# Last output projection of a two-layer decoder trunk: 512 weight columns per matmul instead of 256

## The reference

```python
def branch_b(h, w_in, w_out):
    z = h @ w_in
    q, k, v, gate = jnp.split(z, [B_WIDTH, 2 * B_WIDTH, 3 * B_WIDTH], axis=-1)
    o = stick_breaking_attention(q, k, v).astype(h.dtype)
    return (o * jax.nn.silu(gate)) @ w_out
...
def reference(x, meta_tokens, rel_bias, w_in_a, sinks_a, w_out_a, w_in_b, w_out_b, ln_g, ln_b):
    ...
    h = jnp.concatenate([meta, x], axis=1)
    for i in range(DEPTH):
        j = i // N_MIXERS
        if i % N_MIXERS == 0:
            y = branch_a(h, w_in_a[j], sinks_a[j], w_out_a[j], rel_bias)
        else:
            y = branch_b(h, w_in_b[j], w_out_b[j])
        h = layer_norm(DEEPNORM_ALPHA * h + y, ln_g[i], ln_b[i])
    return h[:, N_META:]
```

## Time and profile before

| what | us |
|---|---|
| median of 3 runs | 966.68 |
| lowest and highest | 965.02, 967.41 |
| span of the profiled execution | 963.3 |
| last output projection, first to last matmul, in that span | 857.8 to 952.4 |
| from the last matmul to the end of the span | 10.9 |

### The profile page before, as it was taken

The page is one execution under the profiler, slowest core; times in us unless marked ns, Lnnn a source line. Parts: engine busy times, 40 slices in busy tenths (PEclk is TensorE's granted clock), DMA queues, the critical chain, the costliest instruction groups (busy, mean ns, idle before and its releaser), DMA issues.

```text
span 963.3 us, 18988 instructions
## 1 busy us (share of the span) xinstructions
PE 928.8 (96%) x7592; PEld 891.9 (93%) x7592; DVE 554.6 (58%) x721; ACT 436.2 (45%) x716; POOL 64.1 (7%) x88
## 2 busy tenths in 40 slices
PE   5999999999999999898999999999999999999995
PEld 5998999999998999898999999999999999999995
DVE  4466566567555666696736455454545546455556
ACT  5456555455645433345445353445335353543330
POOL 2220232032010000011000000000000000000000
PEclk9999999999999999989999999999999999999998
DMA  8755653564343344413554443434344343444532
GB/s 280 237 154 183 210 154 119 149 204 134 129 163 132 131 175 175 175 45 132 195 181 149 152 152 139 166 133 175 132 169 174 131 168 137 174 152 178 206 119 88
DMA packets 24595, 152.99 MB, mean 159 GB/s; under 512 B 3392, under 2 KB 3408, under 8 KB 7792
## 3 DMA queue, kind: packets, MB, share of 16 engines
q1 hardware_dynamic: 20736, 140.52, 40.3%
q0 software_dynamic: 2960, 7.63, 4.1%
q10 hardware_dynamic: 864, 4.33, 1.2%
HBM read 150.28 MB, written 2.18 MB: 158 GB/s over the span
## 4 chain that ended last, share of the span: by engine, by line
PE 88%; DVE 5%; DMA 3%; ACT 1%; issue 1%; SPq 0%; DVEq 0%; ACTq 0%
PE bank L245 72%; DMA raw<-chunks 3%; PE bank L333 2%; PE bank L534 2%; DVE w_lo L820 2%; PE bank L294 2%; ACT w_hi L558 1%; PE bank L314 1%; PE bank L450 1%; PE bank L399 1%; DVE h L1056 1%; PE bank L416 0%; PE bank L405 0%; PE bank L447 0%; PE bank L309 0%
## 5 line engine op out<-in xcount | busy, mean ns | idle before, releaser
L245 PE MATMUL bank<-x_hi,w_hi 128*128 128x272 f32 (+1 forms) x1536 | 446.2, 291 | 16.1 <-DVE w_lo L840 10.4
L245 PE MATMUL bank<-x_hi,w_lo 128*128 128x272 f32 (+1 forms) x1536 | 441.5, 287 | 0.0
L245 PE MATMUL bank<-x_lo,w_hi 128*128 128x272 f32 (+1 forms) x1536 | 441.2, 287 | 0.0
L820 DVE TENSOR_TENSOR w_lo<-raw,w_hi 128x2048 fp32r<-128x2048 f32 x130 | 303.4, 2339 | 218.8 <-ACT w_hi L558 218.6
L558 ACT ACTIVATE w_hi<-raw 128x2048 fp32r<-128x2048 f32 x130 | 248.3, 1911 | 214.3 <-PE bank L245 122.7
L245 PEld LDWEIGHTS bank<-x_hi,w_hi 128*128 128x128 f32 x1536 | 291.6, 190 | 22.4 <-DVE x_lo L826 10.9
L245 PEld LDWEIGHTS bank<-x_hi,w_lo 128*128 128x128 f32 x1536 | 291.2, 190 | 0.0
L245 PEld LDWEIGHTS bank<-x_lo,w_hi 128*128 128x128 f32 x1536 | 291.0, 189 | 0.0
L245 PE MATMUL bank<-og_hi,w_hi 128*128 128x272 f32 x256 | 74.9, 293 | 0.3 <-DVE og_lo L927 0.3
L245 PE MATMUL bank<-og_hi,w_lo 128*128 128x272 f32 x256 | 74.1, 289 | 0.0
L245 PE MATMUL bank<-og_lo,w_hi 128*128 128x272 f32 x256 | 73.7, 288 | 0.0
(11 more groups left out here) (199 smaller groups left out, 1042.0 us busy)
## 6 DMA issues: line engine op xcount, KB each, us to landing
raw<-chunks SPq DMA_DIRECT2D x130, 1024.0 KB, 4.8
work<-bias_table POOLq DMA_DIRECT2D x8, 512.0 KB, 5.8
work<-bias_table POOLq DMA_DIRECT2D x8, 256.0 KB, 6.8
work<-ln_rows ACTq DMA_DIRECT2D x1, 2048.0 KB, 8.2
out<-work SPq DMA_DIRECT2D x8, 256.0 KB, 2.4
h<-xT ACTq DMA_DIRECT2D x3, 544.0 KB, 12.4
raw<-chunks SPq DMA_DIRECT2D x4, 256.0 KB, 7.6
raw<-chunks SPq DMA_DIRECT2D x2, 512.0 KB, 14.1
```

The costliest lines, as they stand in the source:

```text
L245: last = mm(o, l, r, start=(kt == 0 and n == 0), stop=(kt == KT - 1 and n == 2))
L820: V.tensor_tensor(w_lo[:, slot, :, :], raw[:, half, :, :], w_hi[:, slot, :, :].bitcast(f32), ALU.subtract).then_inc(lo_ready, 1)
```

## The change

The last output projection is tiled as 4 rows of 512 output columns (`RW`) in place of 8 pairs of 256. A chunk now holds 4 contraction tiles x 512 columns; its size, its slots and SP's program stay. A row is 4 chunks (c = 0 to 3), and for each chunk PE runs both token tiles: 12 matmuls of 512 columns each, 24 for a chunk, 96 for a row, 384 for the stage. A new semaphore `quarter_used` tells ACT that chunks 0 to 2 of a row are used up; for chunk 3 it is `tile_full[1]`. The transposes of the residual stand after chunk 1 of row 0, that is after 48 matmuls of 512 columns, where they stood after 48 of 256.

DVE makes one add and one statistics instruction of 512 columns for a row and token tile. Its order for row j is now: low parts of chunks 0, 1 and 2 of row j + 1, then `out_cols` of row j for both tiles, then the low part of chunk 3. The last row (j = 3) goes to banks 2 and 3, one for each token tile, tile by tile as before.

```diff
+RW = 512
+QUARTER = KT // 4
+ROW_ITERS = D // RW
...
-        bn_out = sb("bn_out", [128, 2, D // CW, 6])
+        bn_out = sb("bn_out", [128, 2, ROW_ITERS, 6])
...
-        last_acc = (bank[2:4], bank[4:6])
+        last_acc = bank[2:4]
...
+            def row_quarter(j, c, u, o):
+                for k in range(QUARTER):
+                    kt = QUARTER * c + k
+                    whi, wlo = (w[:, c].rearrange("p a b -> p (a b)")[:, k * RW:(k + 1) * RW] for w in (w_hi, w_lo))
+                    part = slice(u * 128, u * 128 + 128)
+                    terms = ((og_hi, whi), (og_lo, whi), (og_hi, wlo))
+                    for n, (m, w) in enumerate(terms):
+                        last = mm(o, m[:, kt, part], w, start=(kt == 0 and n == 0), stop=(kt == KT - 1 and n == 2))
+                return last
+            def out_rows(j):
+                for c in range(4):
+                    pe.wait_ge(lo_ready, 2 * P_OUT_B + 4 * j + c + 1)
+                    for u in range(2):
+                        if c == 0:
+                            pe.wait_ge(tile_free[u], P_OUT_B + j)
+                        last = row_quarter(j, c, u, acc[u][:])
+                        if c == 3:
+                            last.then_inc(tile_full[u], 1)
+                        elif u == 1:
+                            last.then_inc(quarter_used, 1)
+                    if c == 1 and isinstance(j, int):
+                        residual_rows()
             pe.wait_ge(og_lo_ready, O_A + HALF)
-            project(P_OUT_B, og_hi, og_lo, None, token_major=True, between=residual_rows)
-            project(P_OUT_B + 1, og_hi, og_lo, None, token_major=True)
-            with pe.Fori(1, 3) as j:
-                for p in range(2):
-                    project(P_OUT_B + 2 * j + p, og_hi, og_lo, None, token_major=True)
-            for u in range(2):
-                for P in (N_PAIRS - 2, N_PAIRS - 1):
-                    for kt in range(KT):
-                        if u == 0 and kt % HALF == 0:
-                            pe.wait_ge(lo_ready, 2 * P + kt // HALF + 1)
-                        slot, k = 2 * half_slot(P) + kt // HALF, kt % HALF
-                        part = slice(u * 128, u * 128 + 128)
-                        terms = ((og_hi, w_hi), (og_lo, w_hi), (og_hi, w_lo))
-                        for n, (m, w) in enumerate(terms):
-                            last = mm(last_acc[u][P % 2][:, 0:CW], m[:, kt, part], w[:, slot, k, :],
-                                      start=(kt == 0 and n == 0), stop=(kt == KT - 1 and n == 2))
-                    last.then_inc(last_full, 1)
+            out_rows(0)
+            with pe.Fori(1, ROW_ITERS - 1) as j:
+                out_rows(j)
+            for u in range(2):
+                for c in range(4):
+                    if u == 0:
+                        pe.wait_ge(lo_ready, 2 * P_OUT_B + 4 * (ROW_ITERS - 1) + c + 1)
+                    last = row_quarter(ROW_ITERS - 1, c, u, last_acc[u][:])
+                last.then_inc(last_full, 1)
...
-            with act.Fori(0, 3) as j:
-                for p in range(2):
-                    split_hi(P_OUT_B + 2 + 2 * j + p, 0)
-                    split_hi(P_OUT_B + 2 + 2 * j + p, 1)
+            with act.Fori(0, ROW_ITERS - 1) as j:
+                for c in range(4):
+                    n = 2 * P_OUT_B + 4 * (j + 1) + c
+                    act.wait_ge(raw_loaded[c % 2], 16 * (P_OUT_B + 2 * (j + 1) + c // 2 + 1))
+                    act.wait_ge(*((quarter_used, 3 * j + c + 1) if c < 3 else (tile_full[1], P_OUT_B + j + 1)))
+                    A(w_hi[:, c, :, :], raw[:, c % 2, :, :], ACT.Copy).then_inc(hi_ready, 1)
...
-            def out_cols(u, P):
-                r = f["r"][:, u, bass.ds(CW * (P - P_OUT_B), CW)]
-                dve.wait_ge(tile_full[u], P + 1)
-                V.tensor_tensor(r, acc[u][:, 0:CW], r, ALU.add).then_inc(tile_free[u], 1)
-                dve.wait_ge(tile_free[u], P + 1)
-                V.bn_stats(bn_out[:, u, P - P_OUT_B, :], r).then_inc(summed, 1)
-            with dve.Fori(0, 3) as j:
-                for p in range(2):
-                    P = P_OUT_B + 2 * j + p
-                    for u in range(2):
-                        out_cols(u, P)
-                    split_lo(P + 2, 0)
-                    split_lo(P + 2, 1)
+            def out_cols(u, j):
+                r = f["r"][:, u, bass.ds(RW * j, RW)]
+                dve.wait_ge(tile_full[u], P_OUT_B + j + 1)
+                V.tensor_tensor(r, acc[u][:], r, ALU.add).then_inc(tile_free[u], 1)
+                dve.wait_ge(tile_free[u], P_OUT_B + j + 1)
+                V.bn_stats(bn_out[:, u, j, :], r).then_inc(summed, 1)
+            with dve.Fori(0, ROW_ITERS - 1) as j:
+                P = P_OUT_B + 2 * (j + 1)
+                split_lo(P, 0)
+                split_lo(P, 1)
+                split_lo(P + 1, 0)
+                for u in range(2):
+                    out_cols(u, j)
+                split_lo(P + 1, 1)
             def last_cols(u):
-                for n, P in enumerate((N_PAIRS - 2, N_PAIRS - 1)):
-                    r = f["r"][:, u, CW * (P - P_OUT_B):CW * (P - P_OUT_B + 1)]
-                    dve.wait_ge(last_full, 2 * u + n + 1)
-                    V.tensor_tensor(r, last_acc[u][P % 2][:, 0:CW], r, ALU.add).then_inc(last_rows, 1)
-                    dve.wait_ge(last_rows, 2 * u + n + 1)
-                    V.bn_stats(bn_out[:, u, P - P_OUT_B, :], r).then_inc(summed, 1)
+                r = f["r"][:, u, D - RW:D]
+                dve.wait_ge(last_full, u + 1)
+                V.tensor_tensor(r, last_acc[u][:], r, ALU.add).then_inc(last_rows, 1)
+                dve.wait_ge(last_rows, u + 1)
+                V.bn_stats(bn_out[:, u, ROW_ITERS - 1, :], r).then_inc(summed, 1)
...
+    rows = [w_ob[:, i * RW:(i + 1) * RW] for i in range(ROW_ITERS)]
+    chunks = np.concatenate(
+        [c.reshape(2, HALF, 128, CW).transpose(0, 2, 1, 3).reshape(2, 128, HALF * CW) for c in cols]
+        + [c.reshape(4, QUARTER, 128, RW).transpose(0, 2, 1, 3).reshape(4, 128, HALF * CW) for c in rows])
```

More of the change, by code:

```diff
@@ L162, in trunk @@
         centred, last_full, last_rows = sem("centred"), sem("last_full"), sem("last_rows")
+        quarter_used = sem("quarter_used")
         PT_A, PV_A, O_A = 2 * 3 * A_ITERS, 4 * A_ITERS, 2 * A_ITERS
@@ L1166, in token_rstd @@
             def token_rstd(u):
                 mean, var, y, tmp = (bn_mv[:, u, n:n + 1] for n in range(4))
-                dve.wait_ge(summed, KT - 2 + 2 * u)
+                dve.wait_ge(summed, 2 * (ROW_ITERS - 1) + u + 1)
                 V.bn_aggr(bn_mv[:, u, 0:2], bn_out[:, u, :, :]).then_inc(fin_step, 1)
@@ L1320 @@
         cols += [w_b[:, n * D + i * CW:n * D + (i + 1) * CW] for n in range(4)]
-    cols += [w_ob[:, i * CW:(i + 1) * CW] for i in range(8)]
-    chunks = np.stack([c.reshape(2, HALF, 128, CW).transpose(0, 2, 1, 3) for c in cols]) \
-               .reshape(N_CHUNKS, 128, HALF * CW)
+    rows = [w_ob[:, i * RW:(i + 1) * RW] for i in range(ROW_ITERS)]
+    chunks = np.concatenate(
+        [c.reshape(2, HALF, 128, CW).transpose(0, 2, 1, 3).reshape(2, 128, HALF * CW) for c in cols]
+        + [c.reshape(4, QUARTER, 128, RW).transpose(0, 2, 1, 3).reshape(4, 128, HALF * CW) for c in rows])
     d_loc, d_all = 255 - np.arange(LOC), T - 1 - np.arange(T)
```

## The result

| kernel | median, us | range, us | against before, 95% interval | span, us |
|---|---|---|---|---|
| before (the three runs known and two more) | 966.68 | 965.02 to 968.5 (5 runs) | | 963.3 |
| after | 971.17 | 969.37 to 971.43 (5 runs) | 1.0045 (1.0029 to 1.0061) | 967.4 |

What follows compares the result with a forecast made beforehand. PE, busy 96% of the span, was taken as the bound. Matmuls 0, wait +4.4, slow clock +1.8 and tail +0.6 gave +6.8 us: 973.5, 0.7% slower, range 969.0 to 977.0 (8 in 10).

Steps and rivals of the forecast that it cites:

- The wait at row 1: Before row 1, PE waits for DVE's add to free `acc[0]`, delayed by late residual copies, splits and a load: +4.4 us.
- the fast of its two values: Load of row 1's chunk 2, from issue to its high-part split: 4.81 us taken, 7.27 seen once.
- The clock: After the wait at row 1, PE works for some microseconds at granted clock 0.50: +1.8 us.
- The matmuls: Whole stage: 384 matmuls of 512 columns at p = 236.6 ns replace 768 at 118.3 ns, gain 0.
- the slow-clock row: Earlier trace at granted clock 0.50: 272-column matmuls every 227 ns, exactly 272 / 1.2, speaking against a cost per instruction.
- 0.46 to 0.47 ns a column at all three widths: Matmul cost read from the earlier trace at 128, 256 and 272 columns, giving p = 236.6 ns for 512.
- The first rival: Stage's matmuls: fixed cost of 11.6 ns each, p = 225, stage gains 4.5 us, wait 5.0; total +2.9, 969.6; 9%.
- Later rows: Rows 2 and 3 start without a wait of PE, row 2 with some 0.4 us to spare; nothing added.
- The tail: After the last matmul, an add and a statistics instruction of 512 columns, each about 0.3 us longer: +0.6 us.
- No overhead: Rival for the stage's matmuls: p = 213.3 ns, the longer matmul hiding the weight load; total -1.1 us, 965.6; 3%.
- the strong overlap: Rival for the stage's matmuls: 512 columns at the pace of 256, p = 118.3 ns; 933.8 us; 1%.
- The case without a wait: Rival at row 1: ACT or DVE not held by the residual's copies, only the tail is left; 967.3 us; 10%.

Runs made afterwards that it cites:

- the adds first: Changed kernel with DVE's adds and statistics of both token tiles moved ahead of the low-part split of the next row's chunk 2: 964.59 us, ratio 0.9989.
- the residual early: Changed kernel with the transposes of the residual after chunk 0 of row 0, not chunk 1, DVE's order unchanged: 965.81 us, ratio 0.9992.
- the filled wait: Changed kernel with 12 added matmuls of 512 columns behind row 0 on PE, results unread: 969.21 us, ratio 1.0040.
- the residual late: Changed kernel with the transposes of the residual after chunk 2 of row 0, not chunk 1: 976.01 us, ratio 1.0100.

## Why the prediction was right, and where its sizes were off

**The wait at row 1: right in place, cause and size.** Its releaser, the three splits ahead of it and the late load are in the chain as forecast, and both ways of breaking it (the adds first, the residual early) take away the same 5.7 us with the clock's part. 4.4 was forecast, 4.1 measured. The chain was put at 19.3 us (869.2 to 888.5) and is 887.55 - 868.88 = 18.7. The term that was too large is the 1.24 us from the first transpose to ACT's first copy, read from the earlier trace rows. In the trace of before ACT's program still stood at the wait for DVE's last `og_lo`, and then issued the DMA of the last LayerNorm's parameters:

```profile
863.94 0.42 DVE L1131 TENSOR_TENSOR og_lo<-work,og_hi 128x256 f32 x1 [0.78 <-ACT og_hi L790]
864.40 0.34 ACTq L798 DMA_DIRECT2D work<-ln_rows  x1
```

Only then, at 864.78, came the copies; the row's "<-PE bank L513" names the last event but not what held ACT. With the residual 5.3 us later all that is long done, and the copy starts 869.51 - 868.88 = 0.63 after the first transpose. A distance read from a trace holds for another place only if what lies in it moves too. Against this stands the shorter matmul: it brought the transposes 0.3 us forward but row 0's end 0.6, and so lengthened the wait. That 4.4 came so near to 4.1 is in part these two errors, which offset each other. The load took the fast of its two values: 882.66 - 877.83 = 4.83 from its issue to the split, 4.81 in the forecast.

**The clock: right.** 1.8 forecast from the two gaps in the earlier trace rows, 1.7 measured; the filled wait shows that it is the idle time that costs it.

**The matmuls: the term that was mis-sized.** I took p = 236.6, the same time for each column at every width, and it is 231.7: -1.9 us, not 0. The choice against a fixed cost of 11.6 ns (p = 225) was right, and the slow-clock row that decided it stands. The step that failed is "0.46 to 0.47 ns a column at all three widths": all three widths were at or under 272, two of them read from starts rounded to 0.01 us, and they were carried on to 512. With p = 231.7 in the sum, the forecast would have been 6.8 - 336 x 0.0049 = +5.2 (the 336 as in the prediction), and with the shorter start of the copies, 0.6, it would have been +4.5. The first rival, p = 225 with its wait (+2.9), lay nearer to the measured +4.5 than its chance of 9% said; the truth lay between the two.

**Later rows: right.** No wait before row 2, with 0.5 us to spare; none before row 3.

**The tail: +0.4, forecast +0.6.** Both instructions of 512 columns take 0.69 us, against 0.42 and 0.43 for 256, so each costs 0.26 more and not 0.3; the aggregate over half as many values gives back 0.11 (0.26 against 0.37), where the prediction had under 0.05.

**The other rivals.** No overhead (213.3) and the strong overlap (118.3, of the kind of the Trainium skill's 131 ns in TensorE: Matmul & The Clock Gate, Back-to-back issue gap) are excluded by the same rows: 232 ns for 512 columns, 111.5 for 128 where that page has 81. For the isolated gap the same section has N / 2.4 + 2.5, an estimate of 215.8 ns at 512; this float32r stream stays 16 ns above it. The case without a wait was what the code would have done with one line of DVE's order moved. The time, 971.17, lies in the range from 969.0 to 977.0, and it is slower by more than the 0.3% that the prediction took as its bound: 0.45%, though the interval's lower end, 0.29%, is just at it.

## What to carry to other kernels

When a stage's tile is made larger, look at the first tile: what was placed "after the first half of the first tile" moves with the size, and with it everything that one engine queues behind it. Put the short instruction that releases a bank ahead of long ones that prepare work still a tile away, and read the price of a wait of PE of some microseconds as the wait plus the half-rate matmuls behind it. A wait that appears once, at the edge of a loop, can cost more (here 5.7 us with the slow clock) than the loop's body gains over all its turns (here 1.9).

## What the runs showed of the hardware

- float32r matmuls with a weight load of 128 columns each, at granted clock 1.00: 111.5, 119, 174 and 232 ns for 128, 256, 384 and 512 moving columns. At granted clock 0.50, 427 ns for 512 (in the kernel with the residual late), exactly its columns at 1.2 GHz. The cost above the columns at 2.4 GHz (11.6 ns at 256, 118.3 less 106.7; 14 at 384, 174 less 160; 18.4 at 512, 231.7 less 213.3) thus grows with the width from 256 on and vanishes at the lower clock.
- Before: matmuls of 128, 256 and 128 columns, with a 128-wide weight load each, take 0.34 us together; with 64-wide weights, 256 and 128 columns take 0.18.
- An idle time of 3.9 us brought 3.4 us or so at half rate, and rows 1 to 3 took 1.7 us longer from first to last start; after 9.5 us they took 2.4 longer (964.95 - 896.01 = 68.94 against 66.50); after 1.24 us the clock stayed at 1.00.
